# Prompt attention and paged sample attention of a hybrid decoder layer in one phase, with the prompt's weighing on two column halves

## What is computed

```python
s = jnp.einsum('bqhd,bkhd->bhqk', qi, k).astype(F32) * scale
s = s + ci.transpose(0, 2, 1)[..., None] - cum_t[:, :, None, :]
s = jnp.where((qpos[:, None] >= kpos[None, :])[None, None], s, NEG_INF)
p = jax.nn.softmax(s, axis=-1)
return jnp.einsum('bhqk,bkhd->bqhd', p.astype(v.dtype), v)
```

## Time and profile before

| | us |
|---|---|
| median of 3 runs (lowest, highest) | 4241.34 (4240.11, 4242.53) |
| the profiled execution | 4238.19 |
| its span | 4236.6 |
| PE busy in the span | 3589.8 (85%) |
| DVE busy | 1704.0 (40%) |
| ACT busy | 1395.3 (33%) |
| DMA, mean over the span | 147 GB/s |

### The profile page before, as it was taken

The page is one execution under the profiler, slowest core; times in us unless marked ns, Lnnn a source line. Parts: engine busy times, 40 slices in busy tenths (PEclk is TensorE's granted clock), DMA queues, the critical chain, the costliest instruction groups (busy, mean ns, idle before and its releaser), DMA issues. The chain is left out here.

```text
span 4236.6 us, 65891 instructions
## 1 busy us (share of the span) xinstructions
PE 3589.8 (85%) x21028; PEld 2665.7 (63%) x21028; DVE 1704.0 (40%) x3182; ACT 1395.3 (33%) x2381; POOL 372.3 (9%) x630
## 2 busy tenths in 40 slices
PE   6999799969999957887888477599996968959998
PEld 5888688745555534555555355488874746748887
DVE  3222311154545533333333167533334655653333
ACT  3111200023343312332333045433335655642222
POOL 0000000010000001333333311000000000000000
PEclk9999899979999968999999588699997989979999
DMA  5333522212112058999999645533324334242221
GB/s 146 114 112 134 154 98 100 79 34 41 20 20 40 6 112 252 369 361 350 357 370 373 195 161 196 179 124 124 124 103 154 124 94 143 80 154 84 85 87 68
DMA packets 376243, 627.39 MB, mean 148 GB/s; under 512 B 125225, under 2 KB 175186, under 8 KB 376019
## 3 DMA queue, kind: packets, MB, share of 16 engines
q1 hardware_dynamic: 334242, 488.40, 34.8%
q0 software_dynamic: 41792, 136.48, 9.2%
HBM read 489.52 MB, written 135.22 MB: 147 GB/s over the span
## 5 line engine op out<-in xcount | busy, mean ns | idle before, releaser
L1524 PE MATMUL samp_ps_t<-samp_ident,samp_k_ring 128*128 128x128 f32 x2048 | 306.2, 290 | 119.6 <-DMA samp_k_ring<-cache_k 112.2
L123 PE MATMUL in_ps_z<-in_w_hi,in_u_hi 128*128 128x512 f32 x952 | 374.4, 393 | 38.1 <-DVE in_w_lo L156 38.1
L1524 PEld LDWEIGHTS samp_ps_t<-samp_ident,samp_k_ring 128*128 128x128 f32 x2048 | 230.3, 146 | 270.2 <-issue 132.9
L124 PE MATMUL in_ps_z<-in_w_lo,in_u_hi 128*128 128x512 f32 x952 | 373.4, 392 | 0.0
L125 PE MATMUL in_ps_z<-in_w_hi,in_u_lo 128*128 128x512 f32 x952 | 373.1, 392 | 0.0
L1285 POOL DMA_DIRECT2D samp_v_ring<-cache_v x512 | 275.7, 539 | 533.8 <-issue 531.7
L1393 DVE COPY samp_kt<-samp_ps_t 128x512 f32<-128x512 f32 x256 | 175.2, 689 | 319.5 <-PE samp_ps_t L1524 317.9
L841 PE MATMUL fox_ps_o<-fox_prob,fox_v_one 128*65 128x512 f32 (+3 forms) x640 | 279.1, 533 | 0.0
L710 ACT ACTIVATE fox_prob<-fox_ps_k 128x512 f32<-128x512 f32 (+1 forms) x320 | 170.5, 533 | 258.9 <-DVE fox_ps_k L762 146.1
L1318 ACT COPY samp_kt<-samp_ps_t 128x512 f32<-128x512 f32 x256 | 146.8, 585 | 290.7 <-PE samp_ps_t L1524 290.1
L123 PEld LDWEIGHTS in_ps_z<-in_w_hi,in_u_hi 128*128 128x128 f32 x952 | 180.7, 190 | 77.1 <-issue 28.7
(11 more groups left out here) (365 smaller groups left out, 6774.4 us busy)
## 6 DMA issues: line engine op xcount, KB each, us to landing
samp_k_ring<-cache_k SPq DMA_DIRECT2D x512, 256.0 KB, 6.1
samp_v_ring<-cache_v POOLq DMA_DIRECT2D x512, 256.0 KB, 5.3
tail_a_hi<-a_hi SPq DMA_DIRECT2D x34, 512.0 KB, 5.8
tail_a_lo<-a_lo SPq DMA_DIRECT2D x34, 512.0 KB, 6.0
in_w_stage<-w_in_even SPq DMA_DIRECT2D x64, 256.0 KB, 6.5
lru_u_hi<-u_hi SPq DMA_DIRECT2D x8, 2048.0 KB, 8.0
lru_u_lo<-u_lo SPq DMA_DIRECT2D x8, 2048.0 KB, 13.6
in_x<-x SPq DMA_DIRECT2D x17, 512.0 KB, 3.8
```

The lines of the kernel that those rows point to most:

```text
L123: pe.matmul(out, act_hi, w_hi, start=start, stop=False)
L124: pe.matmul(out, act_hi, w_lo, start=False, stop=False)
L1524: last = pe.transpose(ps_t[:, p, a * PAGE:(a + 1) * PAGE], k_ring[:, r, p, a * P:(a + 1) * P], ident[:, :])
```

## The change

One function `attention`, placed after the preparation phase, replaces both. Its parts are those above, with these differences.

- Step t runs prompt head t, K of sequence t+1 and V of sequence t. `merge` lays the two event lists into one order for all engines, by fixed costs written beside each event, and holds transposes into the page bank apart by 0.85 of those costs. An opening runs K of sequence 0 with the first head's turns; the last step has no K. All is unrolled within a step; a loop runs over pairs of steps.
- Banks: `ps_n` one (a look waits for the maximum of the look before), `ps_k` two, `ps_t` one for pages and flips alike (each waits for the copy of the one before), and one each for `ps_o`, `ps_x`, `ps_s`, `ps_v`.
- Rings: 8 K pages and 8 V pages where there were 16 and 16; `prob` eight where there were four; one buffer for the head's natural q and k, fetched by SP between the pages.
- `weigh` takes two key tiles together, one on columns 0 to 63 and one on 64 to 127 of the array, into two halves of `ps_o`. The column of ones is gone: DVE adds up `prob` in SBUF (`add_up`, 40 a head), and `out` folds the halves and sums `acc` with eight small matmuls.

```diff
+                    if k >= 2:
+                        out.append((0.0, "sum", g, s + k - 2, k - 2))
+                    if k >= 3 and k % 2:
+                        out.append((1.05 * cut_width(k - 3 - B4 * g), "weigh", g, s + k - 3, k - 3))
...
+        def merge(fox, samp):
+
+
+            out, since = [], 9.0
+            whole = sum(e[0] for e in fox) * 0.97, max(sum(e[0] for e in samp), 1e-6)
+            done, at = [0.0, 0.0], [0, 0]
+            while at[0] < len(fox) or at[1] < len(samp):
+                pick = 1 if at[0] == len(fox) or (at[1] < len(samp) and done[1] / whole[1] <= done[0] / whole[0]) else 0
+                if pick == 1 and at[0] < len(fox) and samp[at[1]][1] in ("s_turn", "s_flip") and since < SPACE:
+                    pick = 0
...
+        k_ring = ph.sb("samp_k_ring", [P, 2, KG, W])
+        v_ring = ph.sb("samp_v_ring", [P, KG, 2, W])
...
+        ps_n = ph.ps("fox_ps_n", [P, G])
+        ps_k = ph.ps("fox_ps_k", [P, 2, G])
+        ps_o = ph.ps("fox_ps_o", [P, G])
+        ps_x = ph.ps("fox_ps_x", [P, G])
+        ps_t = ph.ps("samp_ps_t", [P, G])
+        ps_s = ph.ps("samp_ps_s", [P, G])
+        ps_v = ph.ps("samp_ps_v", [P, 4, P])
...
+            def head(t, i, par):
+                step(t, i, par)
+                sp.wait_ge(*normed.at(t))
+                if not static(t + 2, H - 1):
+                    sp.wait_ge(*turned.at(t + 1))
+                    fetch(t + 2, par)
...
+            def add_up(t, i, par, g, s, kt):
+                r = max(kt - B4 * g, 0) * P
+                dve.wait_ge(*exped.at(t, s))
+                if kt == 0:
+                    dve.wait_ge(*(o_turned.at(t, g - 2) if g >= 2 else o_turned.at(t - 1, g + 2)))
+                    dve.tensor_copy(acc[:, g % 2, r:G], prob[:, s % RING, r:G]).then_inc(summed.sem, 1)
+                else:
+                    dve.wait_ge(*summed.at(t, s - 1))
+                    dve.tensor_tensor(acc[:, g % 2, r:G], acc[:, g % 2, r:G], prob[:, s % RING, r:G], ALU.add).then_inc(summed.sem, 1)
...
+                pe.wait_ge(*(maxed.at(t, n - 1) if n else maxed.at(t - 1)))
...
+                pe.wait_ge(*(exped.at(t, s - 2) if s >= 2 else exped.at(t - 1, s - 2 + steps)))
...
+                pe.wait_ge(*exped.at(t, s + 1))
+                for n in range(2):
+                    r = max(kt + n - B4 * g, 0) * P
+                    pe.matmul(ps_o[n * HD:(n + 1) * HD, r:G], v[:, par, kt + n, :], prob[:, (s + n) % RING, r:G], start=kt == 0,
+                              stop=kt + 2 == B4 * (g + 1), skip_group_check=True).then_inc(weighed.sem, 1)
...
+                for b in range(B4):
+                    rows, at = HD if g == 0 and b == 0 else P, slice(b * P, (b + 1) * P)
+                    pe.matmul(ps_x[:, b * P:b * P + HD], o_t[0:rows, at], fold[0:rows, :], start=True, stop=True)
+                    last = pe.matmul(ps_x[:, b * P + HD:b * P + HD + 1], acc[:, g % 2, at], ones[:, :], start=True, stop=True)
...
+                pe.wait_ge(kp_in[n % 2][p], 16 * (b * (NKG // 2) + n // 2 + 1))
+                free = page_bank_read(t, "s_turn", (n, p))
+                if free:
+                    pe.wait_ge(*free)
```

More of the change, by code:

```diff
@@ new lines, in attention @@
+        SPACE = 0.85
+        XU = 16
+        OPEN = XU - 2 - 2 * GQ
+        opening = merge(fox_opening(), samp_events(True, False))
+        events = [merge(fox_events(last), samp_events(not last, True)) for last in (False, True)]
+        ident = ph.sb("ident", [P, P])
+        mask = ph.sb("mask", [P, P])
+        mask_t = ph.sb("mask_t", [P, P])
+        nat = ph.sb("fox_natural", [P, 2, PT, HD])
+        q_a = ph.sb("fox_q_a", [P, 2, SEQ], F32R)
+        q_b = ph.sb("fox_q_b", [P, 2, SEQ], F32R)
@@ new lines, in run, with one, step, ahead @@
+        def run(handlers):
+            def one(t, i, par, listed):
+                for kind, *rest in listed:
+                    if kind in handlers:
+                        handlers[kind](t, i, par, *rest)
+            def step(t, i, par):
+                one(t, i, par, events[static(t, H - 2)])
+            return one, step
+        def ahead(t, i, par, dt):
+            return (t + 1, i + par, 1 - par) if dt else (t, i, par)
+        def set_rows(eng, par, done):
+            eng.memset(k_b[HD:P, par, :].bitcast(F32), 0.0)
+            eng.memset(q_b[HD:P, par, :].bitcast(F32), 0.0).then_inc(done, 1)
+            eng.wait_ge(done, 1)
+            eng.memset(k_b[MROW:MROW + 2, par, :].bitcast(F32), 1.0)
+            eng.memset(q_b[HD:HD + 2, par, :].bitcast(F32), 1.0).then_inc(done, 1)
@@ new lines, in s_score @@
+            def s_score(t, i, par, n):
+                b = t + 1
+                if n % 2 == 0 or (static(b, NB - 2) and n // 2 + 2 >= NVC):
+                    return
+                sp.wait_ge(*s_scored.at(b, n))
+                if n // 2 + 2 < NVC:
+                    load_bias(b, n // 2 + 2)
+                else:
+                    load_bias(b + 1, n // 2 + 2 - NVC)
+            one, step = run({"s_turn": s_turn, "s_score": s_score})
+            one(-1, -1, 1, opening)
+            sp.wait_ge(*turned.at(0))
@@ L1268, in _ @@
+            sp.wait_ge(stored, 16 + 16 * H)
         @block.gpsimd
         def _(pool):
[L1270 to L1287 removed]
@@ new lines, in turn @@
+            def turn(t, i, par, dt, j, u):
+                if not (isinstance(t, int) and t < 0 and j == 0):
+                    pe.wait_ge(*x_free(t, u))
+                t, i, par = ahead(t, i, par, dt)
+                pe.wait_ge(head_in, 32 * (t + 1))
+                pe.sem_inc(pe_passed, 1)
+                for b in range(B4):
+                    last = pe.transpose(ps_x[0:HD, b * P:(b + 1) * P], nat[:, j % 2, (j // 2) * B4 + b, :], ident[:, :])
+                last.then_inc(turned.sem, 1)
```

1229 lines of the change are left out of this document (576 added, 653 removed).

## The result

The changed kernel takes **4284.2 us** (median of 4 runs, 4282.7 to 4293.1) against 4240.7 us of the kernel before: ratio **1.0105, 95% interval 1.0092 to 1.0117**. It is slower by 1%. The prediction was 4108 us with a range from 3990 to 4200.

A forecast was written before the change was run, and what follows sets the result against it. PE bounds the prompt phase, DMA the sample phase. Merged: setup 17, opening 104, seven steps of 161 (137 work, 24 waits) 1127, last step 107, end 11, sum 1366 against 1498.9 us; so 4108 us, range 3990 to 4200.

The forecast's parts named there:

- What bounds the kernel: Two phases, 1498.9 us: PE bounds the prompt phase (DMA 0.14 of its rate), DMA the sample phase (share 1.01).
- PE's work, 137 us: Merged step: TensorE's looks, scores, weighings, tops, outs and sample products sum to 133 us, 137 with the granted clock.
- rival 3: Weighing pairs: the two column halves don't run together, costing 124 us in eight steps; 4232 us, no change; chance 0.04.
- Waits, 24 us: Merged step: PE idles 15 us at looks, 2 at pages, 4.3 at the step's turn, 1.3 + 1 at first top, last out.
- the turn of the step: After a step's last score: the first flip waits for a chain on VectorE and ScalarE, 4.3 us.
- VectorE at 0.65, hidden unless someone waits behind it: Merged step: VectorE's 104 us, sums included, are hidden unless someone waits behind; then 0.69 us for every hand-over.
- The opening, 104 us: Before the steps: 64 page hand-overs at 1.39 us, 89 us, plus 15 for scores, half clock and closing chain.
- Rival 4: Opening and last step: half the clock granted where PE has gaps, adding 29 and some 50 us; 4187 us; chance 0.08.
- Rival 1: Merged steps: the waits cover each other, one third of 24 us left, a step 145 us; 3996 us; chance 0.12.
- Rival 2: Merged steps: all 76 hand-overs to VectorE queue 0.45 us more, a step 195 us; 4380 us; chance 0.08.
- Rival 5: Page loads in the steps: pages come late from the halved ring, 5 us a step; 4143 us; no separate chance given.
- sign of failure: Changed kernel's trace: most PE idle before page transposes behind queued DVE copies, or looks' waits at twice 15 us.

The follow-up runs named there:

- e1: Changed kernel with the prompt weighed as before (65 columns, no VectorE sums, closes by transposes), phases still merged: 4256.4 us, ratio 1.0036.
- e5: Changed kernel with each group's top made ahead of a sum on VectorE and turned by TensorE two scores later: 4224.8 us, ratio 0.9972.
- e6: Changed kernel with VectorE's adding up of the prompt's probabilities left out, halves and closes kept: 4258.0 us, ratio 1.0036.
- e7: Kernel before, phases apart, with only the column halves, VectorE's sums and the new closes added: 4355.7 us, ratio 1.0266.
- e3: Changed kernel with odd pages transposed into a second bank, in the opening alone: 4232.7 us, ratio 0.9986.

## Why the prediction was wrong

**What bounds the kernel: half right.** The two bounds of the earlier trace rows were read rightly, and DMA fell to 0.67 of its rate. What I did not draw from it is that TensorE worked 151 of the 171.8 us that a head and a sequence took together. The prediction laid its prices over the prompt phase once ("0.87 by the same sum", 67 of 77.4 us) and did not check that against the trace, which has 72.7, nor over the sample phase, where 70.3 was priced and 78.4 is measured. 20.3 us of idle time a step was about all that a merge could bring, less what it adds.

**PE's work, 137 us: the step that failed.** It measured 149.7, 89 of the 102 us that seven steps are over. The looks and scores were priced at 32.0 us and took 45.4, the outs at 3.2 and took 7.3, the samples at 70.3 and took 72.7. The weighing came in at 19.6 against 22.5, with the pair at 1.0 us and the halves running together (rival 3 is out). Looks, scores and weighings together, whose shares the counting blurs, were priced at 54.5 and took 65.0.

Most of the error was there before the change. TensorE's own work at full clock is 145.7 us before, 144.2 in e1 and 141.9 after; the same prices give 138 for the kernel before (16.0 + 16.0 + 29.6 + 5.2 + 1.0 + 70.3) and 133 after. So the 4 us that the change saves were forecast nearly right, at 5, and the level was 8 to 9 us too low in both. Set against the 171.8 us of before, which are measured, that false level is most of the 11 us a step that the forecast of 161 gained. The other part of the 12.7 us is the clock, 0.95 in the steps and not 0.97: about 8 us and not 4.

The prices of looks and scores were those of products in a row of their like, while in either kernel many stand behind something else. In the changed kernel:

```profile
1465.75 0.60 PE L1546 MATMUL att_samp_ps_t<-att_ident,att_samp_k_ring 128*128 128x128 f32 x4
1466.11 0.48 PE L1463 MATMUL att_fox_ps_n<-att_fox_k_a,att_fox_q_a 128*128 128x512 f32 x1
1466.43 0.40 PE L1464 MATMUL att_fox_ps_n<-att_fox_k_b,att_fox_q_b 96*128 96x512 f32 x1
```

0.32 us from the first product to the second, where the earlier trace rows have 0.23. Over the seven steps, at the full clock, the median for a look behind page transposes is 0.31 us (101 of them) and behind a score 0.24 (69). I priced the change of mode for the weighings, and not that such a border costs something too. By the number of such pairs these borders are some 3 us a step, an estimate (0.08 us, some 41 times), and not the whole of the 8 to 9. Why a border costs this I did not test, and where the rest comes from stays open. The merge as such is not the reason, since e1 has no more own work than the kernel before.

**Waits, 24 us: right in sum, wrong in place.** 25.6 measured. The looks took 10.7 and not 15, the turn of the step 3.4 and not 4.3, the pages 3.1 and not 2. But the tops took 7.1 where I had 1.3: I had counted one top and left three as free, since their instructions are short. I forgot what stands ahead of them on VectorE: in the example above a turn's low part, a mask and a sum. e5 shows that it was 6 us a step that the order alone could give back, with the clock 59 us in all.

**VectorE at 0.65, hidden unless someone waits behind it:** right as a sentence, too cheap as a price of zero. The sums cost 26 us in all by e6, in the merged order; the sums, halves and closes together cost 115 us in a phase of their own by e7.

**The opening, 104 us: wrong through the clock.** 156.4. I had the page's hand-over as the pace and gave the K-only stage's 0.85 of the clock to it. One bank instead of several made gaps of 0.8 us after each page, and with them the clock was granted at half for most of it. e3 gives the bank back and gets 102 us. Rival 4 had this and was priced at 29 us; its own terms, 64 × 0.43 and the scores (16 × 1.00 and 8 × 0.43), come to 47 us at the full clock, so that half the clock can add up to 47. The opening alone lost 52. Its chance was put at 0.08, and in the opening it came true. For the last step rival 4 had up to 50 us; with the end it measured 134.5 against 118, at 0.80 of the clock.

**The range.** The upper end allowed 173 us a step, and 4187 was the sum with rival 4, but the measured steps alone (+102 us) come to 4210, and the opening and the last step add 68 more. Two errors of the same sign, the work and the clock, were treated as if only one could come.

**Rivals.** Rival 1 (waits cover each other) is out, the sum of waits stayed. Rival 2 had the right engine and the wrong size: hand-overs queue behind VectorE, but at the tops and not at all 76. It put the turn to slower at 181 us a step; the kernel is slower at 175.6 already, through the opening and the last step. Rival 5: no wait for a page's load stands among the larger ones in the steps.

**What would show it.** Of the signs that were named, a pair of weighings within 1.2 us, DMA near 0.6, 10.7 us before the looks, few waits for pages and 3.4 us before the first flip all came close, and neither sign of failure appeared. Only the step's period missed. No sign asked for TensorE's own work, which was the term that failed.

## What to carry to other kernels

Before two phases are merged, add up the busiest engine's own work over both, from the trace of the kernel before: the merge can save little but that engine's idle time, and a price list for the kernel after is worth nothing until it gives back the kernel before. Give a merged order slack at each hand-over that stands behind a busy in-order engine: make a small result early, use it late, keep users of one bank apart; in this kernel that, with one bank given back in the opening and the halves undone, was worth 196 us, and turned 1% slower into 3.6% faster. Judge an edit that frees one wait only after looking for the new wait that takes its place: spreading the looks gave 7 us alone and, with the rule that keeps them apart, 63 us once two others were gone.

## What was not expected of the hardware

- Adding 256 small products (512 passes) to the opening shortened it from 156.4 to 131.4 us, with the granted clock going from 0.58 to 0.99.
- The same step's instructions took 150 us of TensorE's time interleaved (clock 0.95) and 211 us one list behind the other (clock 0.73); at full clock by the same estimate, 142 and 147 us.
- A product with one moving column took 0.20 us, each with weights of its own, one with 64 columns 0.25 us.
- With the weighing's halves next to it, nearly every other line of TensorE's work was a little longer (page transposes 32.7 against 30.3 us a step, looks 23.7 against 22.8, scores 21.7 against 20.6), in part through the clock (0.95 against 0.96).
